# The first norm's squares and roots in the modulation's phase, its gates' bounds behind it, and rows of sample and prompt waited for apart

## The reference

```python
mod = (silu(cond) @ w_mod[l] + b_mod[l])           # 6 sections of 1024
sh1, sc1, g1, sh2, sc2, g2 = split(mod, 6)
h = x * rsqrt(mean(x * x) + EPS) * norm1_g[l] * (1 + sc1) + sh1
...
# layer 0: HGRN2 heads (gated recurrence) and windowed attention on h
q, zf, zb, v, zg, aq, ak, av = split(h @ w_in)
gates: log(lb + (1 - lb) * sigmoid(z)),  (1 - lb) * sigmoid(-z)   # lb from a softmax of hgrn_lb
# layer 1: RG-LRU; each layer ends in PEER, a retrieval of 128 experts' rows for each token
```

## Time and profile before

| | us |
|---|---|
| median of 3 runs (4239.04 to 4241.42) | 4240.4 |
| the profiled execution | 4238.9 |
| its span | 4237.2 |

### The profile page before, as it was taken

One profiled execution on the slowest core, in us unless ns is written; L12 is line 12 of the kernel. 1 busy time (PEld: TensorE's weight loads), 2 busy tenths in 40 slices (PEclk: granted clock), 3 DMA queues, 4 the chain that ended last, 5 costly groups with the idle time before them and its releaser, 6 DMA issues.

```text
span 4237.2 us, 46965 instructions
## 1 busy us (share of the span) xinstructions
PE 3006.9 (71%) x15312; PEld 1087.8 (26%) x15312; DVE 3127.5 (74%) x7614; ACT 1325.7 (31%) x3027; POOL 1538.6 (36%) x1356
## 2 busy tenths in 40 slices
PE   5898887776766766766799786656667576666665
PEld 3665443221111111111233231122221212221111
DVE  3433874788878888888667777878879787878786
ACT  3321652222212212123486542232423322223111
POOL 0000001344454544444323334433435344434443
PEclk8999999897877978877899888888888888877777
DMA  4102545999999999999888999999999999999997
GB/s 160 44 29 92 184 159 218 364 426 426 427 426 422 424 414 424 412 418 416 324 308 323 368 345 424 426 393 420 386 407 413 396 426 426 427 419 425 426 422 316
DMA packets 229274, 1494.40 MB, mean 353 GB/s; under 512 B 26394, under 2 KB 49738, under 8 KB 56872
## 3 DMA queue, kind: packets, MB, share of 16 engines
q0 software_dynamic: 185792, 1342.45, 77.0%
q1 hardware_dynamic: 35364, 133.29, 8.4%
q10 hardware_dynamic: 7880, 15.76, 1.0%
HBM read 1488.02 MB, written 3.38 MB: 352 GB/s over the span
## 4 chain that ended last, share of the span: by engine, by line
DMA 26%; DVE 22%; PE 19%; issue 11%; ACT 5%; POOL 1%; DVEq 1%; ACTq 0%; POOLq 0%
DMA trunk_ring<-in_uv,trunk_index 24%; PE trunk_acc L2189 9%; DVE trunk_ring L1856 5%; DVE trunk_diag L1865 3%; DMA trunk_wbuf<-in_w_lru 2%; PE trunk_qp L2100 2%; POOL trunk_ring L1352 1%; PE trunk_q L2139 1%; PE trunk_qp L2226 1%; DVE trunk_onehot L1827 1%; DVE trunk_onehot L1831 1%; DVE trunk_pick L1834 1%; PE trunk_q L2226 1%; PE trunk_acc L2226 1%; DVE trunk_work L1792 1%
## 5 line engine op out<-in xcount | busy, mean ns | idle before, releaser
L2189 PE MATMUL trunk_acc<-trunk_ring,trunk_diag 64*64 64x512 f32 x10240 | 1696.0, 760 | 1015.5 <-DVE trunk_diag L1865 944.1
L1352 POOL DMA_INDIRECT trunk_ring<-in_uv,trunk_index x1280 | 1502.5, 1174 | 2061.0 <-PE trunk_acc L2189 1880.0
L1856 DVE CUSTOM_DVE_ANT_0 trunk_ring<-trunk_ring,HY 128x1024 f32<-128x1024 f32 x1280 | 1561.6, 1222 | 455.6 <-DMA trunk_ring<-in_uv,trunk_index 432.2
L1440 ACT ACTIVATE trunk_acts<-trunk_dots 128x1 f32<-128x1 f32 x1280 | 256.9, 202 | 2220.0 <-DVE trunk_dots L1856 2216.3
L2189 PEld LDWEIGHTS trunk_acc<-trunk_ring,trunk_diag 64*64 64x64 f32 x10240 | 336.7, 154 | 2197.6 <-DVE trunk_diag L1865 1885.6
L1865 DVE TENSOR_SCALAR trunk_diag<-ident,trunk_acts,trunk_gate 128x128 f32<-128x128 f32 x1152 | 395.5, 343 | 117.2 <-ACT trunk_acts L1440 117.1
L2146 PE MATMUL trunk_qp<-HT,trunk_wbuf 128*128 128x512 f32 x448 | 271.5, 690 | 0.0
L1440 ACT ACT_TABLE_LOAD x138 | 177.1, 1283 | 2.4
L1433 ACT ACTIVATE trunk_tmp<-trunk_acc 64x512 f32<-64x512 f32 x264 | 155.5, 589 | 6.4 <-PE trunk_acc L2189 3.4
L2146 PEld LDWEIGHTS trunk_qp<-HT,trunk_wbuf 128*128 128x128 f32 x448 | 72.2, 202 | 210.5 <-issue 210.5
L426 POOL COPY hgrn_Vm<-hgrn_V 64x640 f32<-64x640 f32 x8 | 5.7, 715 | 277.1 <-ACT hgrn_V L456 276.9
(11 more groups left out here) (334 smaller groups left out, 3305.3 us busy)
## 6 DMA issues: line engine op xcount, KB each, us to landing
trunk_wbuf<-in_w_q SPq DMA_DIRECT2D x24, 1024.0 KB, 9.2
att_wm<-in_w_mod SPq DMA_DIRECT2D x11, 2048.0 KB, 8.0
trunk_ring<-in_uv,trunk_index POOLq DMA_INDIRECT x1280, 16.8
watt<-in_w_mod SPq DMA_DIRECT2D x9, 2048.0 KB, 8.2
trunk_wbuf<-in_w_lru SPq DMA_DIRECT2D x16, 1024.0 KB, 15.1
trunk_wbuf<-in_w_rg SPq DMA_DIRECT2D x8, 1024.0 KB, 13.6
mod_wmod<-in_w_mod SPq DMA_DIRECT2D x3, 2048.0 KB, 13.8
hgrn_wqvg<-in_w_hgrn_qvg SPq DMA_DIRECT2D x4, 1536.0 KB, 6.4
```

Source lines behind the costliest of these rows:

```text
L1352: pool.indirect_dma_start(ring[:, slot, :], None, uv[:, :], bass.IndirectOffsetOnAxis(ap=index[:, u % 2, s:s + 1], axis=0), element_offset ...
L1440: act.activation(acts[:, j:j + 1], dots[:, j:j + 1], ACT.Gelu_apprx_tanh).then_inc(act_done, 1)
L1856: dve.tensor_tensor_reduce(u_rows, u_rows, HY[:, b, :], 1.0, 0.0, ALU.mult, ALU.add, dots[:, j:j + 1]).then_inc(dot_done, 1)
L2189: last = pe.matmul(acc[acc_of(u)][c * HALF:(c + 1) * HALF, r * 512:(r + 1) * 512], diag[rows, g % NDIAG, rows], ring[rows, slot, D + c * 5 ...
```

## The change

The squares, the root and the reciprocal of the first norm move from `norm_parts` into the modulation's phase: ScalarE makes them behind its last copy, VectorE takes the reciprocal ahead of L258, with new tiles there and a tile rs0 that lives throughout. In the heads' phase `norm_parts` keeps scaling, transposes and copies. The four row DMAs now have a semaphore for the sample and one for the prompt, and go in the order scale and shift of the sample, scale and shift of the prompt; a block's scaling waits for its own two. ScalarE and VectorE make the lower bounds behind their parts of the norm. The rest of the diff passes rs through the calls.

```diff
-def norm_parts(sb, sem, pre, X, H, HT, ident, AB, ab_landed, ab_target, junk, tp):
-    ss = sb(pre + "ss", [P, NB])
-    rt = sb(pre + "rt", [P, NB])
-    rs = sb(pre + "rs", [P, NB])
-    squared, rooted, inverted = sem(pre + "squared"), sem(pre + "rooted"), sem(pre + "inverted")
+def norm_parts(sem, pre, X, H, HT, ident, AB, ab_landed, rs, tp):
...
     def act(eng):
         for b in range(NB):
-            if b:
-                eng.wait_ge(squared, b)
-            eng.activation(junk, X[:, b, :], ACT.Square, accum_out=ss[:, b:b + 1]).then_inc(squared, 1)
-        eng.wait_ge(squared, NB)
-        eng.activation(rt[:, :], ss[:, :], ACT.Copy, scale=1.0 / D, bias=EPS).then_inc(rooted, 1)
-        eng.wait_ge(rooted, 1)
-        eng.activation(rt[:, :], rt[:, :], ACT.Sqrt).then_inc(rooted, 1)
-        for b in range(NB):
...
     def dve(eng):
-        eng.wait_ge(rooted, 2)
-        eng.reciprocal(rs[:, :], rt[:, :]).then_inc(inverted, 1)
-        eng.wait_ge(inverted, 1)
-        eng.wait_ge(ab_landed, ab_target)
         for b in range(NB):
             c = cond_of(b)
+            eng.wait_ge(ab_landed[c], 32)
...
 def modulation
+        junk = ps("junk", D)
+        ss, rt = sb("ss", [P, NB]), sb("rt", [P, NB])
+        squared, rooted, inverted = sem("squared"), sem("rooted"), sem("inverted")
...
                 act.wait_ge(x_in, 32)
+                for b in range(NB):
+                    if b:
+                        act.wait_ge(squared, b)
+                    act.activation(junk[:, :], X[:, b, :], ACT.Square, accum_out=ss[:, b:b + 1]).then_inc(squared, 1)
+                act.wait_ge(squared, NB)
+                act.activation(rt[:, :], ss[:, :], ACT.Copy, scale=1.0 / D, bias=EPS).then_inc(rooted, 1)
+                act.wait_ge(rooted, 1)
+                act.activation(rt[:, :], rt[:, :], ACT.Sqrt).then_inc(rooted, 1)
...
                     add_bias(i)
+                dve.wait_ge(rooted, 2)
+                dve.reciprocal(rs[:, :], rt[:, :]).then_inc(inverted, 1)
+                dve.wait_ge(inverted, 1)
                 dve.wait_ge(chunk_read, FIRST)
...
 def hgrn
-                load_mod(sp, io, AB[:, 0, :, :], 0, 1, mod_in)
-                load_mod(sp, io, AB[:, 1, :, :], 0, 0, mod_in)
+                for c in range(2):
+                    for i in range(2):
+                        lo = c * LAYERS * 6 * D + (1 - i) * D
+                        sp.dma_start(AB[:, i, c, :], broadcast_rows(io["mod_rows"], lo, D)).then_inc(mod_in[c], 16)
...
             def _(act):
+                n_act(act)
                 act.wait_ge(lb_step, 2)
                 act.activation(lbe[:, :, :, :], lbe[:, :, :, :], ACT.Exp).then_inc(lb_exp, 1)
-                n_act(act)
...
                 dve.sem_inc(head_done, 1)
+                n_dve(dve)
                 c = Count(dve, lb_step)
...
                 dve.tensor_scalar(oml[:, :, :], lb[:, :, :], -1.0, 1.0, ALU.mult, ALU.add).then_inc(lb_ready, 1)
-                n_dve(dve)
...
 def build
+        rs = ctx.enter_context(nc.sbuf_tensor("rs0", [P, NB], F32))
         HY = ctx.enter_context(nc.sbuf_tensor("HY", [P, NB, D], F32))
```

More of the change, by code:

```diff
@@ L169, with modulation @@
 LO = 32
-def modulation(nc, X, HT, ident, cond2, io):
+def modulation(nc, X, HT, ident, cond2, rs, io):
     def body(sb, ps, sem):
@@ L277, in modulation, with hgrn @@
     phase(nc, "mod", body)
[L280 to L288, removed]
+def hgrn(nc, X, HT, YT, watt, ident, rs, io):
     def body(sb, ps, sem):
@@ L322, in body @@
         D0, D1, D2, D3 = (ps(f"D{i}", 1024) for i in range(4))
-        mod_in, lb_in, gn_in, watt_in = sem("e_mod_in"), sem("lb_in"), sem("gn_in"), sem("watt_in")
-        n_act, n_dve, n_pe, h_stored, n_stored = norm_parts(sb, sem, "e_", X, YT, HT, ident, AB, mod_in, 64, D2[:, :], [D0, D1])
+        mod_in = [sem(f"e_mod_in{i}") for i in range(2)]
+        lb_in, gn_in, watt_in = sem("lb_in"), sem("gn_in"), sem("watt_in")
+        n_act, n_dve, n_pe, h_stored, n_stored = norm_parts(sem, "e_", X, YT, HT, ident, AB, mod_in, rs, [D0, D1])
         consts, czero = sem("consts"), sem("czero")
@@ L1045, in attention, with even_mixer @@
     phase(nc, "att", body)
-def even_mixer(nc, X, HT, YT, ident, cond2, io):
+def even_mixer(nc, X, HT, YT, ident, cond2, rs, io):
     with ExitStack() as ctx:
         watt = ctx.enter_context(nc.sbuf_tensor("watt", [P, KD, 6 * P], F32))
-        hgrn(nc, X, HT, YT, watt, ident, io)
+        hgrn(nc, X, HT, YT, watt, ident, rs, io)
         attention(nc, X, HT, YT, watt, ident, cond2, io)
@@ L2450, in build @@
         constants(nc, iota16)
-        modulation(nc, X, HT, ident, cond2, io)
-        even_mixer(nc, X, HT, HY, ident, cond2, io)
+        modulation(nc, X, HT, ident, cond2, rs, io)
+        even_mixer(nc, X, HT, HY, ident, cond2, rs, io)
         trunk(nc, X, HY, HT, ident, iota16, io)
```

## The result

The changed kernel takes 4281.0 us (median of 5 runs) where the kernel before takes 4240.4 (now a median of 5 runs too): a ratio of 1.0102, interval 1.0089 to 1.0115. It is slower by 41 us; forecast were 11 us less. The profiled execution's span is 4278.6.

A forecast was written before the change was run, and what follows sets the result against it. Most of the last-ending chain lies in the trunk, untouched; the change shortens the first 90 us. First scaling 11.15 us earlier takes the profiled 4238.9 to 4227.8, plus 1.5 for the median: 4229.3 us, range 4225 to 4236.

The forecast's parts named there:

- the new tile moves all others: Rival: rs0 shifts the gathers' ring to 32 past a multiple of 256; 1% slower gathers cost 33 us; chance 0.06.
- Rows 7 do not bear it out for loads into SBUF: Attention's weight loads into tiles on 256 and 96 past it had medians 8.2 and 8.0 us: odd start no slower.
- the sum: First scaling 11.15 us earlier, everything behind it keeping durations and order: forecast 4229.3 us, a gain of 0.26%.
- estimate from that page for an 8 KB row: Gathers off a 256-byte start: 33 transactions for 32 in each row, 3.1% or 101 us, time 4330.
- The squares: Modulation's phase: start behind ScalarE's last copy at about 31.8, root's end 7.62 us later at 39.46, no table load.
- VectorE's cover: Modulation's phase: VectorE asks for the root only behind its last bias addition at 41.32, 1.86 us to spare.
- The reciprocal: Modulation's phase: ahead of L258 on VectorE, it delays store, barrier and the mixer's DMAs by 0.22 us.
- The bounds' exponential: Mixer: bounds' chain behind ScalarE's fifth copy takes under 3 us, hidden in ScalarE's 9.06 us idle before first projection's release.
- The second row: Mixer's start: the sample's second row lands 6.1 us after its issue, at 51.85; bounds 4.0 and 8.0 us.
- the first scaling: Mixer: VectorE's first scaling starts at 51.90 instead of 63.05, bounds 49.8 and 53.8.
- case of a late rise: TensorE's clock rising 3 us into the projection would cost 1.5 us; 2.5 us allowed both ways in all.
- the rise does not move along with the work: TensorE's clock monitor runs freely, so an earlier start does not shift the rise; sum stays 4229.3, with scatter.

The follow-up runs named there:

- e4: Kernel before with an unused tile of 64 bytes ahead of HY, so the ring starts 64 past a multiple of 256: 4283.0 us, ratio 1.0111.
- e5: Kernel before with an unused tile of 128 bytes ahead of HY, so the ring starts 128 past a multiple of 256: 4277.1 us, ratio 1.0091.
- e1: Changed kernel with 56 unused columns behind rs0, so HY, HT and all phases' tiles move by 256 bytes, not 32: 4225.5 us, ratio to before 0.9974.
- e3: Changed kernel with an unused 224-byte tile ahead of the gathers' ring, putting the trunk's tiles alone back on 256: 4224.8 us, ratio to before 0.9966.
- e2: Kernel before with only an unused tile of 20 bytes a partition where the change puts rs0: 4290.9 us, ratio 1.0139.
- e8: e1 with the lower bounds ahead of the norm again, one profiled execution: first row DMA to first scaling 9.96 us (17.95 before, 5.50 changed kernel).

## Why the prediction was wrong

**The step that failed** is in the rival "the new tile moves all others": "Rows 7 do not bear it out for loads into SBUF", and with it the chance of 0.06. So the sum put the gathers' slow-down at nothing. What the rival said was right: the ring's start, the gathers, 33 us for each 1%. Measured are 1.9% fewer MB in equal time and 56.8 us more from the first gather to the last. What was wrong was to let two medians decide. They were 8.0 and 8.2 us in the earlier trace rows, 0.2 us apart, which is 2.4%, while the rival decided at 0.34%: the rows could not resolve it; the landings of att_wm alone spread from 7.8 to 9.7 us. In the changed kernel both tiles have moved, to 128 and 32 past, and the profile's part on DMA issues has nearly the same numbers:

```profile
att_wm<-in_w_mod SPq DMA_DIRECT2D x11, 2048.0 KB, 8.1
...
watt<-in_w_mod SPq DMA_DIRECT2D x9, 2048.0 KB, 8.1
```

So these loads show nothing of the start in either kernel, while gathers that hold the engines at 99.0% do. Whether the loads are free of the cost or it is too small to be seen in a landing time was not tried.

The Trainium skill (DMA: Bandwidth & Descriptors, How a descriptor splits into AXI transactions) gives the step as 256 bytes: a transaction has to start at a multiple of 256. It says so of reads; here it was the start of what is written that moved, and e4, e5 and e1 agree with the step: 64 and 128 past cost, 256 does not. The prediction's estimate from that page for an 8 KB row, 3.1%, is more than the 1.5 to 1.9% of MB measured.

**The steps that held.** The squares began at 31.92 and the root ended at 39.54 (39.46 foretold), under VectorE's cover to 41.47, and no table load stood ahead of the squares. The reciprocal cost 0.20 (0.22). The bounds' exponential ran at 67.30, and ScalarE still waited 9.72 us for the projection.

**Sizes that were off.** The second row landed 5.1 us after its issue, not 6.1, so the first scaling came at 50.86, not 51.90. The clock did take part: it was low for 4.5 us of the projection and cost 2.2 us, where the prediction's case of a late rise had 3 and 1.5. The prediction's "the rise does not move along with the work" did not hold: the rise behind the first transposes lies between 60 and 62 where it lay between 77 and 78, so 15 to 18 us earlier, with the first transposes 12.2 earlier (53.46, 65.65 before).

**What of the gain was luck.** With the ring on a multiple of 256 (e1, e3) the gain is 0.26% (0.14 to 0.38) and 0.34% (0.22 to 0.45), where the forecast was 0.26%. The direction and the size were right. That it came out so near is partly luck: the landing was 1 us better than the sum had it and the clock 2.2 us worse, and the phases behind scatter by more than that. The first gather starts at 685.5 to 693.2 us in the seven profiled executions with the old order and at 673.2 to 679.6 in the three with the whole change, so the 13.6 us of the changed kernel are one draw out of 6 to 20. Part of the scatter is in attention, which the change does not touch: from its first DMA to the first gather it takes 329.2 us in the kernel before (364.0 to 693.2) and 324.5 in the changed one (355.1 to 679.6), but 324.5 in e2 (361.0 to 685.5) and 329.2 in e8 (356.3 to 685.5).

**What stays open.** Why the price of the start varies between 0.9 and 1.4%, why attention takes one of two lengths, and by what the chip's memory or engines make the start cost anything.

## What to carry to other kernels

A new tile is also an edit of every address behind it: when a small tile is added ahead of a buffer that saturated gathers write, keep that buffer's start on a multiple of 256, by a pad as in e1 and e3. Before a rival is put down by two rows, compare their scatter with the point from which the rival decides. And when several chains lead to one start, each one's worth is what it lies behind the next, not its own length.

## What the runs showed of the hardware

Indirect gathers of 8 KB rows at 99% of the DMA engines moved 413 to 414 MB in 1000 us into a ring that starts at a multiple of 256 bytes and 406 to 408 MB where it starts 32, 64, 128 or 224 past one. VectorE's passes over the same ring took 1221 to 1223 ns in the mean at either start. An unused tile of 20 bytes made a kernel of 4241 us slower by 1.4% (1.2 to 1.6). TensorE's granted clock, at 1.00 from 62 to 63 with TensorE idle, was at 0.50 from 64 on and came up again only 4.5 us into the projection.
